# Last layer norm in token order: x transposed into six PSUM banks right behind its sums, norm and affine applied on the way out

## The reference

```python
def layer_norm(x, g, b):
    xf = x.astype(jnp.float32)
    mu = jnp.mean(xf, -1, keepdims=True)
    var = jnp.mean(jnp.square(xf - mu), -1, keepdims=True)
    return ((xf - mu) * lax.rsqrt(var + LN_EPS) * g + b).astype(x.dtype)

def trunk_layer(x, mod, p, lam_init, ctx):
    ...
    h = swiglu(adaln(x, 2), p['ffn_w_in'][1], p['ffn_w_out'][1])
    x = layer_norm(DEEPNORM_ALPHA * x + 0.5 * m(8) * h, p['ln_g'][2], p['ln_b'][2])
    return x, ctx_out
```

## Time and profile before

| what | us |
|---|---|
| median of 3 runs | 2542.89 |
| lowest and highest | 2540.56, 2545.5 |
| the profiled execution, its own time | 2548.7 |
| its span, first to last instruction | 2545.9 |
| mean granted PE clock | 0.971 of full |

### The profile page before, as it was taken

One profiled execution on the slowest core, in us unless ns is written; L12 is line 12 of the kernel. 1 busy time (PEld: TensorE's weight loads), 2 busy tenths in 40 slices (PEclk: granted clock), 3 DMA queues, 4 the chain that ended last, 5 costly groups with the idle time before them and its releaser, 6 DMA issues.

```text
span 2545.9 us, 56113 instructions
## 1 busy us (share of the span) xinstructions
PE 2388.8 (94%) x23644; PEld 2234.5 (88%) x23644; DVE 1367.8 (54%) x2311; ACT 1038.2 (41%) x1686; POOL 332.9 (13%) x326
## 2 busy tenths in 40 slices
PE   6999999999978889999999999999998888899997
PEld 5899989889967779999989899998998777899997
DVE  3434365476478655444443344655766775654444
ACT  3333244355634435333343323434564443353332
POOL 0000032000033304000120002210001341120001
PEclk8999999999999999999999999999999999999998
DMA  8875734233300024563557765333232000334441
GB/s 291 263 221 179 219 93 132 84 94 91 104 7 4 29 62 131 156 188 111 171 184 216 228 192 159 100 108 95 87 87 75 4 4 29 97 106 126 128 131 55
DMA packets 468246, 308.27 MB, mean 121 GB/s; under 512 B 15282, under 2 KB 427420, under 8 KB 467868
## 3 DMA queue, kind: packets, MB, share of 16 engines
q1 hardware_dynamic: 467728, 304.60, 39.9%
q10 hardware_dynamic: 268, 0.09, 0.0%
HBM read 301.25 MB, written 3.41 MB: 120 GB/s over the span
## 4 chain that ended last, share of the span: by engine, by line
PE 85%; DVE 8%; issue 2%; ACT 2%; DMA 1%; POOL 1%; SPq 0%; DVEq 0%; ACTq 0%; POOLq 0%
PE acc L888 22%; PE acc L890 21%; PE acc L889 21%; PE pb L1285 5%; PE acc L1285 2%; PE pb L965 2%; PE pb L973 1%; PE pb L1212 1%; DVE w_lo L2307 1%; PE pb L980 1%; PE pb L888 1%; DMA modx<-in_w_mod 1%; DVE merged L2588 0%; PE pb L1232 0%; DVE gr L2689 0%
## 5 line engine op out<-in xcount | busy, mean ns | idle before, releaser
L888 PE MATMUL acc<-xm_hi,w_hi 128*128 128x384 f32 x2288 | 786.5, 344 | 28.4 <-DVE xm_lo L2317 23.7
L2307 DVE TENSOR_TENSOR w_lo<-raw,w_hi 128x1024 fp32r<-128x1024 f32 (+2 forms) x432 | 531.9, 1231 | 510.6 <-ACT w_hi L1716 502.0
L890 PE MATMUL acc<-xm_hi,w_lo 128*128 128x384 f32 x2288 | 773.4, 338 | 0.0
L889 PE MATMUL acc<-xm_lo,w_hi 128*128 128x384 f32 x2256 | 762.2, 338 | 0.0
L1716 ACT ACTIVATE w_hi<-raw 128x1024 fp32r<-128x1024 f32 (+2 forms) x432 | 446.3, 1033 | 319.6 <-PE acc L890 214.4
L888 PEld LDWEIGHTS acc<-xm_hi,w_hi 128*128 128x128 f32 x2288 | 436.4, 191 | 59.0 <-issue 43.3
L890 PEld LDWEIGHTS acc<-xm_hi,w_lo 128*128 128x128 f32 x2288 | 435.6, 190 | 0.0
L889 PEld LDWEIGHTS acc<-xm_lo,w_hi 128*128 128x128 f32 x2256 | 430.5, 191 | 0.5
L888 PE MATMUL acc<-h_hi,w_hi 128*128 128x384 f32 x704 | 238.8, 339 | 0.0
L890 PE MATMUL acc<-h_hi,w_lo 128*128 128x384 f32 x704 | 237.1, 337 | 0.0
L889 PE MATMUL acc<-h_lo,w_hi 128*128 128x384 f32 x704 | 237.0, 337 | 0.0
(11 more groups left out here) (391 smaller groups left out, 3480.3 us busy)
## 6 DMA issues: line engine op xcount, KB each, us to landing
raw<-in_ffn_w_in SPq DMA_DIRECT2D x176, 512.0 KB, 4.1
modw<-in_w_mod SPq DMA_DIRECT2D x69, 1024.0 KB, 6.7
raw<-in_w_in SPq DMA_DIRECT2D x114, 512.0 KB, 4.1
raw<-in_ffn_w_out SPq DMA_DIRECT2D x64, 512.0 KB, 4.3
raw<-in_w_up SPq DMA_DIRECT2D x24, 512.0 KB, 3.5
raw<-in_ffn_w_out SPq DMA_DIRECT2D x26, 384.0 KB, 3.5
raw<-in_w_out SPq DMA_DIRECT2D x16, 512.0 KB, 4.4
modx<-in_w_mod SPq DMA_DIRECT2D x3, 1024.0 KB, 9.3
```

The source lines that it names most:

```text
L888: pe.matmul(out, lhs[0], rhs[0], start=first, stop=False)
L889: pe.matmul(out, lhs[0], rhs[1], start=False, stop=False)
L890: return pe.matmul(out, lhs[1], rhs[0], start=False, stop=last)
L2307: done(dve.tensor_tensor(w_lo[:, c % SPL, 0:w], raw[:, c % RAW, 0:w], w_hi[:, c % SPL, 0:w].bitcast(F32), ALU.subtract), lo_done)
```

## The change

The last layer norm of the last layer leaves the channel-major path. The rest of the program is as it was, except for two loads in SP's queue.

- PE: right behind the last `token_sums` it transposes x, as it stands before the norm, into six banks (`acc[0]` to `acc[3]`, `pb[1]`, `pb[2]`), with no wait. The two spreads and the transposes at the end are gone.
- DVE: the sixteen passes over x and three copies are gone. After the reciprocal it makes `shift_rstd` = `delta_c` * `rstd_c` (128 x 3) and then, for half rows 0, 1, 2 and 4, two instructions each: (bank + `delta_c`) * g into `xrows` (`moved`), and `xrows` * `rstd_c` + b (`scaled_row`).
- ACT: `plain_norm` and three copies are gone. For half rows 3 and 5 it writes bank * `rstd_c` + `shift_rstd` into `xrows` (`y_scaled`).
- POOL: for half rows 3 and 5, `xrows` * g, then + b, in place.
- g and b are needed along the free axis now: SP loads row 2 of `ln_g` and of `ln_b` of layer 1 (4 KB each) into all 128 partitions of `gb_rows`, in the first of `modw`'s three buffers, 512 KB each on the SBUF side. They stand in the queue of the second FFN's weights at chunk `first + RAW`, behind a wait for ("w", 7).
- SP: three stores of 512 KB instead of one of 512 KB and one of 1024 KB: the prompt after two half rows of DVE, tokens 0 to 127 of the sample after half rows 2 (DVE) and 3 (POOL), tokens 128 to 255 after 4 (DVE) and 5 (POOL).

```diff
+            gb_rows = modw[:, 0, :, :].rearrange("p a c -> p (a c)").rearrange("p (r d) -> p r d", r=2)
+            shift_rstd = ln_st[:, 9:12]
...
+        def y_bank(n):
+            return (acc + [pb[1], pb[2]])[n]
+        def y_half(of, n):
+            return of[:, n // 2, n % 2 * 512:n % 2 * 512 + 512]
...
             (SP, loop over the chunks)
+                        elif n == first + RAW:
+                            wait_group(l, sy, ("w", KD - 1))
+                            sy.wait_ge(st_out, since(l, st_out, 32))
+                            for i, name in enumerate(("ln_g", "ln_b")):
+                                sy.dma_start(gb_rows[:, i, :], I[name][l, 2:3, :].to_broadcast([128, D])).then_inc(par_in, 16)
...
-                sy.wait_ge(y_done, 2)
+                sy.wait_ge(y_rest, 2)
                 sy.dma_start(O["y_prompt"][0], xrows[:, 0, :]).then_inc(y_out, 16)
-                sy.wait_ge(y_done, NCH)
-                sy.wait_ge(y_rest, NCH)
-                sy.dma_start(O["y_sample"][0].rearrange("(c p) d -> p c d", p=128), xrows[:, 1:3, :]).then_inc(y_out, 16)
+                for c in range(1, NCH):
+                    sy.wait_ge(y_rest, c + 2)
+                    sy.wait_ge(y_pool, c)
+                    sy.dma_start(O["y_sample"][0, (c - 1) * 128:c * 128, :], xrows[:, c, :]).then_inc(y_out, 16)
...
             (PE, in layer_norm)
+                        if s == 2 and l == DEPTH - 1:
+                            for n in range(2 * NCH):
+                                for k in range(4):
+                                    mm = pe.transpose(y_bank(n)[:, k * 128:(k + 1) * 128],
+                                                      x[:, 4 * (n % 2) + k, n // 2 * 128:n // 2 * 128 + 128], ident)
+                                mm.then_inc(y_t, 1)
+                            return
...
             (ACT)
-                    def plain_norm(s):
-                        for m in range(KD):
-                            act.wait_ge(n_ready, since(l, n_ready, KD * s + m + 1))
-                            done(act.activation(x[:, m, :], x[:, m, :], ACT.Identity, scale=par[:, 72 + KD * s + m:73 + KD * s + m],
-                                                bias=par[:, 96 + KD * s + m:97 + KD * s + m]), x_ready)
+                    def y_scaled(n):
+                        c = n // 2
+                        act.wait_ge(y_t, n + 1)
+                        act.wait_ge(stat_ready, since(l, stat_ready, 10))
+                        done(act.activation(y_half(xrows, n), y_bank(n)[:, :], ACT.Identity, scale=rstd_c[:, c:c + 1],
+                                            bias=shift_rstd[:, c:c + 1]), y_done)
...
             (POOL, at its end)
+                pool.wait_ge(par_in, 16 * (14 * DEPTH + 2))
+                for i, n in enumerate((3, 5)):
+                    pool.wait_ge(y_done, i + 1)
+                    h = n % 2
+                    link(pool.tensor_tensor(y_half(xrows, n), y_half(xrows, n), gb_rows[:, 0, h * 512:h * 512 + 512], ALU.mult))
+                    done(pool.tensor_tensor(y_half(xrows, n), y_half(xrows, n), gb_rows[:, 1, h * 512:h * 512 + 512], ALU.add), y_pool)
...
             (DVE, behind the reciprocal)
+                        def moved(n):
+                            dve.wait_ge(y_t, n + 1)
+                            h, c = n % 2, n // 2
+                            link(dve.scalar_tensor_tensor(out=y_half(xrows, n), in0=y_bank(n)[:, :], scalar=delta_c[:, c:c + 1],
+                                                          in1=gb_rows[:, 0, h * 512:h * 512 + 512], op0=ALU.add, op1=ALU.mult))
+                        def scaled_row(n):
+                            h, c = n % 2, n // 2
+                            done(dve.scalar_tensor_tensor(out=y_half(xrows, n), in0=y_half(xrows, n), scalar=rstd_c[:, c:c + 1],
+                                                          in1=gb_rows[:, 1, h * 512:h * 512 + 512], op0=ALU.mult, op1=ALU.add), y_rest)
+                        done(dve.tensor_tensor(shift_rstd, delta_c, rstd_c, ALU.mult), stat_ready)
+                        dve.wait_ge(par_in, 16 * (14 * DEPTH + 2))
+                        for n in (0, 1, 2, 4):
+                            moved(n)
+                            scaled_row(n)
```

More of the change, by code:

```diff
@@ L456, in build @@
         tile_sum, tok_sums, stat_ready, spread_t = (sem(n) for n in ("tile_sum", "tok_sums", "stat_ready", "spread_t"))
-        var_ready, std_done, n_ready, x_ready = (sem(n) for n in ("var_ready", "std_done", "n_ready", "x_ready"))
+        var_ready, std_done, n_ready, y_pool = (sem(n) for n in ("var_ready", "std_done", "n_ready", "y_pool"))
         lam_in, lam_b, lam_dot, lam_exp, lam_done = (sem(n) for n in ("lam_in", "lam_b", "lam_dot", "lam_exp", "lam_done"))
@@ L838, in _ @@
                             load_mod(sy, l + 1, p + 1)
-                sy.wait_ge(y_done, 2)
+                sy.wait_ge(y_rest, 2)
                 sy.dma_start(O["y_prompt"][0], xrows[:, 0, :]).then_inc(y_out, 16)
-                sy.wait_ge(y_done, NCH)
-                sy.wait_ge(y_rest, NCH)
-                sy.dma_start(O["y_sample"][0].rearrange("(c p) d -> p c d", p=128), xrows[:, 1:3, :]).then_inc(y_out, 16)
+                for c in range(1, NCH):
+                    sy.wait_ge(y_rest, c + 2)
+                    sy.wait_ge(y_pool, c)
+                    sy.dma_start(O["y_sample"][0, (c - 1) * 128:c * 128, :], xrows[:, c, :]).then_inc(y_out, 16)
                 sy.wait_ge(st_out, 32 * DEPTH)
-                sy.wait_ge(y_out, 32)
+                sy.wait_ge(y_out, 16 * NCH)
             @block.tensor
@@ L1688, in _ @@
                     ffn(1)
-                pe.wait_ge(x_ready, KD)
-                for n in range(2 * NCH):
-                    if n >= 4:
-                        pe.wait_ge(y_done, n - 3)
-                    for k in range(4):
-                        mm = pe.transpose((acc[0], acc[1], pb[1], pb[2])[n % 4][:, k * 128:(k + 1) * 128],
-                                          x[:, 4 * (n % 2) + k, n // 2 * 128:n // 2 * 128 + 128], ident)
-                    mm.then_inc(y_t, 1)
             @block.scalar
@@ L2140, in _ @@
                     if l == DEPTH - 1:
-                        plain_norm(2)
-                for n in range(NCH):
-                    act.wait_ge(y_t, n + 1)
-                    done(act.activation(xrows[:, n // 2, n % 2 * 512:n % 2 * 512 + 512],
-                                        (acc[0], acc[1], pb[1], pb[2])[n % 4][:, :], ACT.Copy), y_done)
+                        for n in (3, 5):
+                            y_scaled(n)
             @block.gpsimd
@@ L2364, in norm_residual, with y_rows @@
                             shift_tile(s, KD - 1)
+                    def y_rows():
+                        def moved(n):
[12 more added lines that the diff above has]
+                            scaled_row(n)
                     def layer_norm(s):
@@ L2374, in layer_norm @@
                         done(dve.reciprocal(rstd_c, ln_st[:, 16:19]), stat_ready)
+                        if s == 2 and l == DEPTH - 1:
+                            y_rows()
+                            return
                         dve.wait_ge(spread_t, since(l, spread_t, 3 * s + 2))
@@ L2925, in _ @@
                     ffn(1)
-                for n in range(NCH, 2 * NCH):
-                    dve.wait_ge(y_t, n + 1)
-                    dve.tensor_copy(xrows[:, n // 2, n % 2 * 512:n % 2 * 512 + 512],
-                                    (acc[0], acc[1], pb[1], pb[2])[n % 4][:, :]).then_inc(y_rest, 1)
         nc.multi_engine_barrier(all_engines(), sems_to_clear=range(sems[0].num, sems[-1].num + 1))
```

## The result

The changed kernel takes 2529.85 us in the median of 6 runs (2522.88 to 2532.87) against 2542.11 of 6 runs of the kernel before (2540.49 to 2545.5). The ratio is 0.9949, with an interval of 0.9938 to 0.996 (it is worked out over all the runs and so isn't the quotient of the two medians). The profiled execution took 2532.87 and has a span of 2531.1, with a mean granted clock of 0.975.

The account below looks back on a forecast made before the run. PE is busy 94%, but behind its last sums a hardly overlapping chain bounds the end. Saving 5.5 us ahead of the last store and 1.4 within it gives 2542.89 - 6.9 = 2536.0 us, range 2531.5 to 2540.5.

Parts of the forecast that it names:

- turns between POOL and DVE: Last norm: `scaled_row` and POOL's instructions wait for each other in full, costing POOL two turns of 0.75 us, about 1.5.
- PE's part: 24 transposes right behind the token sums at full clock, 1.1 us a bank, banks readable from 2523.4 to 2528.9.
- POOL's chain: POOL's four instructions on half rows 3 and 5, last of all compute: about 7 us, from 2527.6 to 2534.6.
- DVE, ACT and the store: Last norm: DVE 0.75 us an instruction, ACT 0.80 a half row; last store 2.6 to landing instead of 4.0.
- The loads: g and b in the second FFN's weight queue: there by 2238 with the chunk, 18 us of cover, costing nothing.
- What stays: Statistics, closing barrier and everything ahead of the sums' end at 2522.2 unchanged; moving over 2 us would make the prediction wrong.
- No turns: Rival at the end: POOL undisturbed by DVE, ending at 2533.2; gain 8.4 us, 2534.5; chance 20%.
- The last store doesn't get shorter: Rival: half the data still takes 4.0 us to land; gain 5.5, 2537.4; 17% together with slow POOL.
- POOL is slower than in proportion: Rival: POOL at 1.7 us an instruction instead of 1.36, costing as much as the long store; 17% together with it.
- Slower: Rival: 128 partitions reading the same 4 KB delay the weights queued behind; at 36 us of loads 2550; chance 3%.
- The clock falls at once: Rival: clock falls in the token sums, a bank takes 1.76 us; gain 5.0, 2537.9; chance 10%.

Follow-up runs that it names:

- the other order: Changed kernel with ACT and POOL on half rows 1 and 3, DVE on the rest, the sample stored in four 256 KB pieces: ratio 0.9955, tail 13.0 us.
- one input: Changed kernel with DVE's `scaled_row` reading the PSUM bank instead of `xrows`, so one SBUF input: POOL's chain 5.30 us, tail 14.3.
- one store: Changed kernel with `y_sample` stored in one transfer of 1024 KB at the end: POOL's end to span's end 5.79 us, tail 16.3.
- late transposes: Changed kernel with PE waiting for the reciprocal before it transposes: POOL starts 6.14 us behind the sums, tail 16.5.
- two inputs: Changed kernel with `moved` reading b's row from SBUF instead of the bank, so both DVE instructions have two SBUF inputs: tail 15.7 us.

## Why the prediction was wrong

The sign and the mechanism came out: faster, a chain that POOL ends, turns between POOL and DVE, loads that cost nothing. Two terms were mis-sized, PE's first of all, and what lies ahead of the sums did not stay where it was.

- **PE's part failed, by 2.56 us.** I took a bank of four transposes for eight records, and between 0.9 and 1.5 us I chose 1.1. The text ahead of the prediction also says that transposes show two records each. That is wrong. The sums do show two each, but a transpose shows one: both kernels have 24 transposes, and the rows have 16 and 8 records now and three rows of 8 before. So one row of 8 in the earlier trace rows was two banks, 0.88 each at half clock. At full clock a bank takes 1.78 / 4 = 0.45 (2517.25 to 2519.03, confirmed by the doubled transposes), and even my lower bound of 0.9 lay above the truth. Half row 3 is read 1.9 behind the sums instead of 4.5, and POOL starts 2.84 behind them instead of 5.4. The bound failed because both ends rested on one reading of a count.
- **POOL's chain was 0.55 us too long.** I had 7.0, and it takes 6.45. About half of that is the instruction alone, 1.26 instead of 1.36 in proportion from 384 columns. The other half is the price of a turn. I had two turns at DVE's whole 0.75. All four of POOL's instructions met a `scaled_row`, but that cost the first 0.17 and the others 0.33. Each time POOL ends 1.12 us behind DVE's end, where it takes 1.26 alone, and DVE ends 0.55 behind POOL's, where it takes 0.75 alone. So 0.14, 0.20 and the 0.08 between two of POOL's instructions pass during the wait, and 0.33 of the 0.75 are left. I could have read that in the earlier trace rows: POOL's 1.78 ends 0.69 behind DVE's end (0.83 alone), and DVE's 1.07 ends 0.41 behind POOL's (0.56 alone).
- **DVE, ACT and the store were right.** 0.75 for each of DVE's instructions, 0.78 for ACT (0.80), 4.4 from POOL's end to the end of the span, 1.25 and 1.37 us for half the data of the last store in the two kernels that change it alone. Also right was that POOL is last: DVE ends 1.1 us earlier.
- **The loads were right.** They went out at 2225.83, ahead of the weight chunks, all had landed by 2235, and ACT takes a chunk at 2251.21 without having waited for it. That is a cover of 16 us or more, where I had 18.
- **What stays did not stay.** The end of the sums moved by 4.8 us in the first pair of traces, over the 2 us that I had named. Part of it is there before any changed instruction has run. The program's first norm has its reciprocal at 350.98 to 352.21 in all ten traces of the changed kernel and its variants, and at 352.65 to 353.73 in the three of the kernel before (also with the loads or the split store alone). The means are 1.8 us apart. So this goes with the program, and its cause stays open. The rest differs between executions of either: from that reciprocal to the last one the kernel before takes 2164.7 to 2170.8 and the changed one with its variants 2160.6 to 2168.4. In the first pair most of the rest lies in layer 1, between the last reciprocal ahead of its mixing and the one of the next norm. This piece takes 637.7 in the trace of before, 634.9 in that of the changed kernel, and 631.1 to 634.2 in four others (the loads alone, the split store alone, the changed kernel twice). The mean granted clock from 1940 to 2212, inside that piece, was 0.93, 0.94 and 0.96 in the four, so the clock goes with it. That it is the cause was not tried.

In sum: the tail gives 2.56 + 0.55 = 3.1 more than predicted, which makes 2532.9 from the same start, still inside the range. The first measurement lies another 2.3 lower ahead of the sums and 0.8 for the median of before (2542.11 in the comparison, not 2542.89). Together that is 6.2, the distance of 2536.0 from 2529.85. Taken off the same 2542.89, the mean of the three ratios gives 2533.2, inside the range too. So the mis-sized bank brought the forecast to the edge, and what no term of mine covered took it over. The range was narrow on the low side because all its cases used the same rate for a bank.

Does the change gain anything ahead of the sums? In five comparisons the gain by the ratio differs from that of the tail by 3.0, -1.6, 1.4 (doubled transposes), -2.0 and 0.7 us (the other order), 0.3 in the mean. A lead of 1.8 us in the whole time is neither shown nor excluded by this.

**The rivals.** "No turns" is out: POOL's chain would be 5.30. "The last store doesn't get shorter" is out by two runs, and "POOL is slower than in proportion" by its 1.26. "Slower" is out by the result, and its mechanism by the loads alone. "The clock falls at once" is real. The clock fell in the sums in 5 of 13 traces: two variants of the kernel before (the loads alone, the split store) and three of the changed one (one input, one store, late transposes). With the transposes at their true length it costs the changed kernel some 1.2 to 1.7 us (one store, one input: POOL starts 4.2 and 4.54 behind the sums instead of 2.84), where I had 1.9. The kernel before pays 0.5 to 0.7 for it (tails of 24.2 with the loads alone, and of 23.1 + 1.25 with the split store, instead of 23.7). So the end of the changed kernel depends on the clock more than that of the kernel before.

## What to carry over

Count records against the instructions of the program before a row of xN is used as a unit: here one wrong count moved both bounds of a term to the wrong side, and the range with it. When a chain that ends a kernel is shortened, its worth is best read as a distance inside the trace (here from the last sums to the end of the span), which repeats to 0.1 us where the clock does the same, while whole executions differ by 10. An engine that waits its turn for a shared read doesn't lose the other's whole instruction (0.33 of 0.75 here), and work that needs no shared read fits beside the other engine at no cost, as `moved` does.

## What the runs showed of the chip

- **Turns, in numbers.** In every stretched pair of the changed kernel POOL ends 1.12 us after the DVE instruction that it waited for (2522.21 to 2523.33), and DVE 0.55 after POOL (2523.33 to 2523.88). Alone they cost 1.26 and 0.75. The same two distances, within 0.02, are found with the doubled transposes, the late transposes, the one store, two inputs and the other order, while DVE's instructions last anything from 0.85 to 1.64 there, by how much of POOL's was left. So neither engine gets further beside the other than its first 0.14 or 0.20, which I read as the part before the first element; the runs show the size and not the cause. The Trainium skill (SBUF — State Buffer, "Who interferes with whom") states that a DVE instruction with two SBUF inputs contends with a GpSimd instruction that reads SBUF, for a pair of ports that is locked and not shared out. The runs agree on who meets whom, with one SBUF input (no stretch) and with two (stretch), and on the lock; they add the price.
- **A float32 transpose** of 128 x 128 costs 0.11 us at full clock and 0.22 at half, and leaves one record, where a float32 sum leaves two.
- **The clock can fall while PE is busy.** With the same instructions in front of it, the granted clock went to 0.50 (1.2 GHz) within the one-column sums in 5 executions and held at 1.00 (2.4 GHz) in 8. In the seven of these that belong to the changed kernel and its variants it held through the transposes too, in the changed kernel until three us after them. What decides between the two was not found. It can come back while PE does nothing but transposes: in the run with one store the 1 us stretches from 2511 to 2514 show 0.50, the next one 0.95 and the one behind it 1.00.
- **Stores by size** from SP's queue, issue to landing: 256 KB 2.0 us, 512 KB 2.6, 1024 KB 4.0.
